# Feed-forward activations turned by VectorE squares and by transfers between SBUF tiles, with the weight blocks in a new order

## The chip, the cores and the metric

One core of a Trainium2 chip runs the whole program. TensorE multiplies (its results go to PSUM, eight banks of 128x512 floats), ScalarE and VectorE work element by element, GpSimd takes a few powers, SyncE issues the loads; 16 DMA engines move the data. The metric is the time of one execution on the device in microseconds, the median of several runs.

## The reference, cut to what matters

Two transformer blocks over 256 tokens of width 1024. Four times in it stands the same feed-forward, twice with an RMS norm ahead of it and a factor of one half, twice in the second block:

```python
def swiglu(u, w_gate, w_up, w_down):
    return (jax.nn.silu(u @ w_gate) * (u @ w_up)) @ w_down
```

Its hidden width is 2816. The rest (latent and differential attention, a recurrent and a convolutional mixer, pooling, cross attention to 256 memory tokens) is not touched by the change, apart from the normalization of the memory tokens, which both kernels spread over the first feed-forward.

## The kernel before, in words

All weights come as a stream of 128x1024 float blocks of 512 KB. Each is loaded by SyncE into one of seven raw buffers (`w_raw`), split by ScalarE into a rounded part (`w_hi`, `part_hi`, L650) and by VectorE into the remainder (`w_lo`, `part_lo`, L1223), and used by TensorE as three products, high x high, high x low, low x high (`three`, L2067 to L2069). The split parts lie in a ring of five (`RING`). ScalarE and VectorE call `behind(b)` in the order of the stream: it splits block b + 5, and ScalarE's part waits until TensorE is done with the block whose place it takes. Each engine works through its queue strictly in order, so whatever stands ahead of a split delays it.

A feed-forward (`token_ffn(f, b0)`, f = 0 to 3) has its hidden width in six pieces n: five of 512 and one of 256. For a piece, TensorE computes gate n into PSUM banks 0 and 1 (one for each half t of the tokens) and up n into banks 2 and 3, four weight blocks each. ScalarE takes silu of the gate (`sig`, L737), VectorE multiplies it with the up result (`hidden`, L1402 and L1403) into `hf`, with tokens on the partitions. The down product needs hidden features on the partitions. So TensorE transposes `hf` by an identity in squares of 128x128 into banks 2 and 3 (`turn_h`, L2318), eight a piece and four for the last; ScalarE copies them into `h_hi` (`hidden_hi`, L743), VectorE makes `h_lo` (`hidden_lo`), and four blocks of down n follow. The order of blocks is written into `ffn_place`: for n = 1 to 4 gate n, down n-1, up n, with `turn_h(n-1)` after the second gate block, and at the end gate 5 with up 5 in one (blocks 56 to 59) and the last six down blocks.

In the queues of the first feed-forward stand also the work on the memory tokens (`memory_stats`, `memory_norm`, `turn_memory`, L2242, `memory_gain`), and of the second one a norm of an embedding (`embedding_sum`, `embedding_var`, whose statistics TensorE sums in L2353, before the second half of gate 1). In the third and fourth, `residual_rows` (VectorE, L1526 and L1529) and `residual_in` (ScalarE, L717) stand ahead of the splits of up 0.

Of the kernel before, what the change touches and what calls it, by code (L numbers as in the profile page):

```python
# [12 lines left out]
ACT = mybir.ActivationFunctionType  # L13
# [3 lines left out]
P = 128  # L17
# [36 lines left out]
FFN_LO = (2,) * 5 + (1,)  # L54
FFN_LO_ALL = sum(FFN_LO)


def ffn_place(kind, n, i=0):

    if n == 0 and kind != "D":  # L60
        return i + (4 if kind == "U" else 0)
    if kind == "D":
        return 8 + 12 * n + 4 + i if n < 4 else 60 + i
    if n < 5:
        return 8 + 12 * (n - 1) + (8 if kind == "U" else 0) + i
    return 56 + i
# [118 lines left out]
def build(nc, x_d, first_d, mem_d, pT, prm_d, id_d, cst_d, late_d, row_d, w_d, out):  # L185
    with ExitStack() as ctx:
# [199 lines left out]
        mem_in, p_in, prm_in, cst_in, out_done, ones_set = sems("mem_in p_in prm_in cst_in out_done ones_set")  # L386
        f_sg, f_h, f_t, f_hh, f_hl = sems("f_sg f_h f_t f_hh f_hl")
        xt_ready, xt_ps, ss_ready, rs_ready, dg_ready, rb_ps, rb_ready = sems(
# [251 lines left out]
        def _(act):  # L640
# [79 lines left out]
            def token_ffn(f, b0):  # L720
# [48 lines left out]
                for n in range(1, 5):  # L769
                    behind(b1 + ffn_place("G", n, 0))  # L770
                    behind(b1 + ffn_place("G", n, 1))
                    hidden_hi(n - 1)
                    if f == 0 and n == 4:
                        memory_hi()
                    behind(b1 + ffn_place("G", n, 2))
                    behind(b1 + ffn_place("G", n, 3))
                    sig(n)
                    for i in range(4):
                        behind(b1 + ffn_place("D", n - 1, i))
                        if f == 0 and n in (2, 3) and i == 1:  # L780
                            memory_gain(n - 2)
                    for i in range(4):
                        behind(b1 + ffn_place("U", n, i))
                        if f == 0 and n == 1 and i == 1:
                            memory_norm()
                behind(b1 + 56)
                hidden_hi(4)
                behind(b1 + 57)
# [3 lines left out]
                behind(b1 + 60)  # L792
                hidden_hi(5)
                for i in range(61, 64):
# [407 lines left out]
        def _(dve):  # L1202
# [195 lines left out]
            def token_ffn(f, b0):  # L1398
# [6 lines left out]
                def hidden(n):  # L1405
                    done(b1 + ffn_place("U", n, 3))
                    if n:
                        dve.wait_ge(f_t, FFN_LO_ALL * f + 2 * n)
                    for t in range(2):
                        dve.wait_ge(f_sg, 12 * f + 2 * n + t + 1)  # L1410
                        times(hf[:, t, :], PB[2 + t][:, :], t, sg[:, t, :]).then_inc(f_h, 1)

                def last_hidden():

                    dve.wait_ge(f_t, FFN_LO_ALL * f + 10)
# [25 lines left out]
                for n in range(1, 5):  # L1441
                    if f == 1 and n == 1:
                        embedding_sum()
                    behind(b1 + ffn_place("G", n, 0))
                    behind(b1 + ffn_place("G", n, 1))
                    hidden_lo(n - 1)
# [9 lines left out]
                    behind(b1 + ffn_place("G", n, 3))  # L1456
                    for i in range(4):
# [7 lines left out]
                    for i in range(3):  # L1465
                        behind(b1 + ffn_place("U", n, i))
                    hidden(n)
                    behind(b1 + ffn_place("U", n, 3))
                behind(b1 + 56)
                hidden_lo(4)  # L1470
# [4 lines left out]
                hidden_lo(5)  # L1475
                behind(b1 + 60)
# [578 lines left out]
        def _(pe):  # L2055
# [202 lines left out]
            def token_ffn(f, b0):  # L2258
# [43 lines left out]
                def up(n):  # L2302
                    if n:
                        pe.wait_ge(f_hl, FFN_LO_ALL * f + 2 * n)
                    if f == 0 and n in (2, 3):
                        pe.wait_ge(mem_g, 4 * (n - 1))
                    for i in range(4):
                        front("U", n, i)

                def turn_h(n):  # L2310
                    pe.wait_ge(f_h, 12 * f + 2 * n + 2)
                    if f == 0 and n == 0:
                        pe.wait_ge(prm_in, 32)
                    for k in range(FFN_LO[n]):
                        for j in range(2):
                            for t in range(2):
                                at = j * S + t * P
                                ins = nc.tensor.transpose(PB[2 + k][:, at:at + P], hf[:, t, (2 * k + j) * P:(2 * k + j + 1) * P], ident)  # L2318
                        ins.then_inc(f_t, 1)

                def down(b, n, jp, h):
                    pe.wait_ge(f_hl, FFN_LO_ALL * f + 2 * n + jp + 1)
                    outs = [PB[k] for k in Y_BANK[y][2 * h:2 * h + 2]]
# [24 lines left out]
                for n in range(1, 5):  # L2348
                    gate(n, 0)
                    gate(n, 1)  # L2350
                    if f == 1 and n == 1:
                        pe.wait_ge(pp_sum, 1)
                        nc.tensor.matmul(half(4, 0), ones, pp_sq[:, 0, :], start=True, stop=True).then_inc(pp_stat, 1)  # L2353
                    turn_h(n - 1)
                    gate(n, 2)
                    gate(n, 3)
                    if f == 1 and n == 1:
                        pe.wait_ge(pp_var, 1)
                    for i in range(4):
                        if f == 0 and n in (2, 3) and i == 2:  # L2360
                            turn_memory(n - 2)
                        down(b1 + ffn_place("D", n - 1, i), n - 1, i // 2, i % 2)
                    up(n)
                gate(5, 0)
                turn_h(4)
                gate(5, 1)
                gate(5, 2)
                token_last(place("G", 5, 3), PB[0:2], (6, 7), x_hi, x_lo, f_gu)
                for i, (n, jp, h) in enumerate(FFN_END):
                    if i < 3 or f < 2:  # L2370
                        down(b1 + 60 + i, n, jp, h)
                    if i == 0:
                        turn_h(5)
                    if i == 3 and f < 2:
# [634 lines left out]
```

## Time and profile before

| | before |
|---|---|
| median of 3 runs, us | 1238.38 (1238.14 to 1238.65) |
| span of the profiled execution, us | 1236.5 |
| TensorE busy, us | 1227.8 (99%) |
| TensorE weight load busy, us | 1046.1 (85%) |
| VectorE busy, us | 801.5 (65%) |
| ScalarE busy, us | 672.9 (54%) |
| moved by DMA | 219.93 MB, mean 178 GB/s |

The page gives for each engine the time with an instruction under way. Matmuls overlap in their pipeline, so a matmul's own duration is more than what it adds to the time; the chain of waits and the starts in the timeline show the latter. Idle time is put down to what ended it.

### The profile page before, as it was taken

The page shows a single profiled execution, that of the slowest core. Times are in us where ns is not written, and L with a number is a line of the kernel's source. Part 1 is how long each engine was busy: PE and PEld are TensorE (multiplying, and loading weights), DVE is VectorE, ACT ScalarE, POOL GpSimd, SP SyncE. Part 2 cuts the span into 40 slices and gives each one's busy share as a digit, 9 for nine tenths or more (in the row PEclk, how much of TensorE's full clock was granted, in tenths as well). Part 3 has the DMA queues.
Part 4 walks back from the last instruction along what each step waited for, and adds up shares of the span by engine and source line. Part 5 has one row for each costly group of instructions (what it writes and reads, how often), then busy time and mean ns, then how long its engine had stood idle before and what let it go on. Part 6 is the DMA issues. An engine that isn't in the chain of part 4 may idle for free.

```text
span 1236.5 us, 16493 instructions
## 1 busy us (share of the span) xinstructions
PE 1227.8 (99%) x6444; PEld 1046.1 (85%) x6444; DVE 801.5 (65%) x1186; ACT 672.9 (54%) x1037; POOL 31.0 (3%) x36
## 2 busy tenths in 40 slices
PE   9999999999999999999999999999999999999997
PEld 8888888888888888899978888888888888888886
DVE  6655556878766555568999765755557674755455
ACT  7545546668574444455776646544445754644441
POOL 0000000010000000000001000000001000000000
PEclk9999999999999999999999999999999999999999
DMA  9755555452355555544445633755554443566540
GB/s 361 260 198 189 187 185 198 156 190 87 110 181 190 189 187 187 187 154 162 167 150 171 214 110 118 268 186 189 188 188 158 172 152 120 204 221 192 188 166 34
DMA packets 60892, 219.93 MB, mean 178 GB/s; under 512 B 6672, under 2 KB 8208, under 8 KB 60176
## 3 DMA queue, kind: packets, MB, share of 16 engines
q1 hardware_dynamic: 60528, 218.50, 51.8%
q8 instruction: 51, 0.84, 0.3%
q10 hardware_dynamic: 288, 0.39, 0.1%
q14 instruction: 25, 0.20, 0.1%
HBM read 217.81 MB, written 1.05 MB: 177 GB/s over the span
## 4 chain that ended last, share of the span: by engine, by line
PE 92%; DVE 6%; issue 1%; DMA 0%; ACT 0%; DVEq 0%; ACTq 0%
PE bank L2067 26%; PE bank L2069 26%; PE bank L2068 26%; PE bank L2119 2%; DVE arena L1881 2%; PE bank L2318 2%; PE bank L2120 1%; DVE w_lo L1223 1%; PE bank L2467 1%; PE bank L2428 1%; PE bank L2288 1%; DVE arena L1896 1%; PE bank L2439 1%; PE bank L2422 1%; PE bank L2460 1%
## 5 line engine op out<-in xcount | busy, mean ns | idle before, releaser
L1223 DVE TENSOR_TENSOR w_lo<-w_raw,w_hi 128x1024 fp32r<-128x1024 f32 x389 | 476.5, 1232 | 339.9 <-ACT w_hi L650 339.1
L650 ACT ACTIVATE w_hi<-w_raw 128x1024 fp32r<-128x1024 f32 x389 | 409.2, 1058 | 422.5 <-PE bank L2069 405.4
L2067 PE MATMUL bank<-w_hi,x_hl 128*128 128x512 f32 (+2 forms) x912 | 357.8, 392 | 0.6 <-DVE w_lo L1223 0.6
L2069 PE MATMUL bank<-w_hi,x_hl 128*128 128x512 f32 (+2 forms) x912 | 353.0, 387 | 0.0
L2068 PE MATMUL bank<-w_lo,x_hl 128*128 128x512 f32 (+2 forms) x912 | 352.8, 387 | 0.0
L2069 PEld LDWEIGHTS bank<-w_hi,x_hl 128*128 128x128 f32 x912 | 171.3, 188 | 34.8
L2067 PEld LDWEIGHTS bank<-w_hi,x_hl 128*128 128x128 f32 x912 | 171.4, 188 | 34.6 <-issue 1.3
L2068 PEld LDWEIGHTS bank<-w_lo,x_hl 128*128 128x128 f32 x912 | 171.5, 188 | 32.9
L2067 PE MATMUL bank<-w_hi,h_hi 128*128 128x512 f32 (+1 forms) x364 | 142.0, 390 | 0.0
L2069 PE MATMUL bank<-w_hi,h_lo 128*128 128x512 f32 (+1 forms) x364 | 141.3, 388 | 0.0
L2068 PE MATMUL bank<-w_lo,h_hi 128*128 128x512 f32 (+1 forms) x364 | 141.2, 388 | 0.0
L2069 PEld LDWEIGHTS bank<-w_hi,h_lo 128*128 128x128 f32 x364 | 68.3, 188 | 14.0
L2067 PEld LDWEIGHTS bank<-w_hi,h_hi 128*128 128x128 f32 x364 | 68.4, 188 | 13.8 <-DVE h_lo L1241 0.2
L2068 PEld LDWEIGHTS bank<-w_lo,h_hi 128*128 128x128 f32 x364 | 68.4, 188 | 13.6
L2119 PE MATMUL bank<-x_hl,w_hi 128*128 128x512 f32 x128 | 46.8, 407 | 0.0
L2067 PE MATMUL bank<-x_hl,w_hi 128*128 128x256 f32 x152 | 43.6, 287 | 0.0
L2068 PE MATMUL bank<-x_hl,w_hi 128*128 128x256 f32 x152 | 43.0, 283 | 0.0
L2069 PE MATMUL bank<-x_hl,w_lo 128*128 128x256 f32 x152 | 43.0, 283 | 0.0
L2067 PE MATMUL bank<-m_hi,w_hi 128*128 128x256 f32 x128 | 37.6, 294 | 0.0
L2068 PE MATMUL bank<-m_lo,w_hi 128*128 128x256 f32 x128 | 36.2, 283 | 0.0
L2069 PE MATMUL bank<-m_hi,w_lo 128*128 128x256 f32 x128 | 36.2, 283 | 0.0
L2120 PE MATMUL bank<-x_hl,w_lo 128*128 128x256 f32 x128 | 35.9, 280 | 0.0
(329 smaller groups left out, 1387.8 us busy)
## 6 DMA issues: line engine op xcount, KB each, us to landing
w_raw<-weights_d SPq DMA_DIRECT2D x394, 512.0 KB, 3.3
arena<-ln_rows_d SPq DMA_DIRECT2D x3, 1024.0 KB, 5.5
arena<-weights_d SPq DMA_DIRECT2D x4, 512.0 KB, 5.2
arena<-late_d SPq DMA_DIRECT2D x1, 1056.0 KB, 7.3
arena<-first_d SPq DMA_DIRECT2D x2, 512.0 KB, 5.5
xs<-x_d SPq DMA_DIRECT2D x2, 512.0 KB, 7.2
kv_mem<-mem_d SPq DMA_DIRECT2D x1, 1024.0 KB, 7.3
out_d<-kv_mem SPq DMA_DIRECT2D x3, 256.0 KB, 2.1
```

What stands on the lines that cost most here:

```text
L650: nc.scalar.activation(w_hi[:, slot(b), :], w_raw[:, b % RAW, :], ACT.Copy).then_inc(hi_ready, 1)
L1223: nc.vector.tensor_tensor(w_lo[:, slot(b), :], w_raw[:, b % RAW, :], w_hi[:, slot(b), :].bitcast(F32), ALU.subtract).then_inc(lo_ready, 1)
L1881: ins = nc.vector.scalar_tensor_tensor(conv[:, c, :], src, w, conv[:, c, :], ALU.mult, ALU.add)
L1896: nc.vector.tensor_tensor(flat(conv), flat(conv), flat(tap_buf[j]), ALU.add).then_inc(tap_added, 1)
L2067: nc.tensor.matmul(out, wh, xh, start=start, stop=False, skip_group_check=True)
L2068: nc.tensor.matmul(out, wh, xl, start=False, stop=False, skip_group_check=True)
L2069: return nc.tensor.matmul(out, wl, xh, start=False, stop=stop, skip_group_check=True)
L2119: nc.tensor.matmul(bank[:, :], wh, flat(x_hl[:, k, :, :]), start=k == 0, stop=k == TILES - 1, skip_group_check=True)
L2120: return nc.tensor.matmul(bank[:, 0:S], wl, x_hl[:, k, 0, :], start=False, stop=k == TILES - 1, skip_group_check=True)
L2288: ins = nc.tensor.matmul(PB[t][:, :], xa[:, c, t * P:(t + 1) * P], wa[:, b, o], start=c == 0 and kind == "high", stop=c == 7 and kind == " ...
L2318: ins = nc.tensor.transpose(PB[2 + k][:, at:at + P], hf[:, t, (2 * k + j) * P:(2 * k + j + 1) * P], ident)
L2422: ins = nc.tensor.matmul(half(n % 2, t), q_mla[0:QK, h, t * P:(t + 1) * P], k_mla[0:QK, h, :], start=True, stop=True)
```

## The change

For the pieces n = 0 to 4, TensorE's transposes go. VectorE turns `hf` in squares of 32x32 (two instructions a piece, one for each t) into `h_quads`. A square is then on the right columns but within its own quarter of the partitions, so ScalarE issues 16 transfers a piece from its own DMA queue (`hidden_across`), each of 32 partitions x 1 KB from a quarter of `h_quads` to a quarter of `h_turned`, both in SBUF. `hidden_hi` waits for all 16 (`h_in`) and copies from there to `h_hi`, in two instructions of 128x512, and `hidden_lo` makes `h_lo` likewise. The piece of 256 is still turned by TensorE (`turn_last`).

The order of blocks becomes gate n, up n, down n-1. ScalarE issues the transfers of piece n after the split behind the first block of down n-1, and copies to `h_hi` after the fourth; for n = 0 the issues come after the first block of gate 1 and the copy after `sig(1)`. The memory tokens' steps move within the first feed-forward, and `turn_memory` waits for the products instead of for `h_lo`.

```diff
     if kind == "D":
-        return 8 + 12 * n + 4 + i if n < 4 else 60 + i
+        return 8 + 12 * n + 8 + i if n < 4 else 60 + i
     if n < 5:
-        return 8 + 12 * (n - 1) + (8 if kind == "U" else 0) + i
+        return 8 + 12 * (n - 1) + (4 if kind == "U" else 0) + i
...
+        h_quads = [region(ARENA - 8 * S if f < 2 else 16 * S, QUADS, 2, 4 * QUAD)[0] for f in range(4)]
+        h_turned = [region(ARENA - 4 * S if f < 2 else 20 * S, QUADS, 2, 4 * QUAD)[0] for f in range(4)]
...
+        def hidden_from(f, t):
+
+            return h_turned[f][:, :, t, :].rearrange("p q (c s) -> p q c s", s=QUAD)
+
+        def hidden_to(h, t):
+
+            return h[:, 0:4, t * P:(t + 1) * P].rearrange("p c (q s) -> p q c s", s=QUAD)
...
                 def hidden_hi(n):
-                    for k in range(FFN_LO[n]):
-                        act.wait_ge(f_t, FFN_LO_ALL * f + 2 * n + k + 1)
-                        j = 2 * k + (4 if n == 5 else 0)
-                        nc.scalar.activation(flat(h_hi[:, j:j + 2, :]), PB[2 + k][:, :], ACT.Copy).then_inc(f_hh, 1)
+                    act.wait_ge(h_in, 16 * QUADS * QUADS * (TURNED * f + n + 1))
+                    if n:
+                        done(b1 + ffn_place("D", n - 1, 3))
+                    for t in range(2):
+                        nc.scalar.activation(hidden_to(h_hi, t), hidden_from(f, t), ACT.Copy).then_inc(f_hh, 1)
+
+                def hidden_across(n):
+                    act.wait_ge(h_turn, 2 * (TURNED * f + n + 1))
+                    for q in range(QUADS):
+                        for r in range(QUADS):
+                            nc.scalar.dma_start(h_turned[f][r * QUAD:(r + 1) * QUAD, q, :, :], h_quads[f][q * QUAD:(q + 1) * QUAD, r, :, :]
+                                                ).then_inc(h_in, 16)
...
                 for n in range(1, 5):
-                    behind(b1 + ffn_place("G", n, 0))
-                    behind(b1 + ffn_place("G", n, 1))
-                    hidden_hi(n - 1)
-                    if f == 0 and n == 4:
-                        memory_hi()
-                    behind(b1 + ffn_place("G", n, 2))
-                    behind(b1 + ffn_place("G", n, 3))
+                    for i in range(4):
+                        behind(b1 + ffn_place("G", n, i))
+                        if n == 1 and i == 0:
+                            hidden_across(0)
+                        if f == 0 and n == 2 and i == 1:
+                            memory_norm()
+                        if f == 0 and n == 4 and i == 1:
+                            memory_hi()
                     sig(n)
+                    if n == 1:
+                        hidden_hi(0)
+                    for i in range(4):
+                        behind(b1 + ffn_place("U", n, i))
                     for i in range(4):
                         behind(b1 + ffn_place("D", n - 1, i))
+                        if i == 0:
+                            hidden_across(n)
                         if f == 0 and n in (2, 3) and i == 1:
                             memory_gain(n - 2)
...
+                    hidden_hi(n)
...
                 def hidden(n):
                     done(b1 + ffn_place("U", n, 3))
-                    if n:
-                        dve.wait_ge(f_t, FFN_LO_ALL * f + 2 * n)
                     for t in range(2):
                         dve.wait_ge(f_sg, 12 * f + 2 * n + t + 1)
                         times(hf[:, t, :], PB[2 + t][:, :], t, sg[:, t, :]).then_inc(f_h, 1)
+                    if TURNED * f + n:
+                        dve.wait_ge(h_in, 16 * QUADS * QUADS * (TURNED * f + n))
+                    for t in range(2):
+                        dve.wait_ge(f_h, 12 * f + 2 * n + t + 1)
+                        nc.vector.transpose(h_quads[f][:, :, t, :].rearrange("p r (c s) -> p c r s", s=QUAD),
+                                            hf[:, t, :].rearrange("p (c r j) -> p c r j", r=QUADS, j=QUAD)).then_inc(h_turn, 1)
...
-                    for k in range(FFN_LO[n]):
-                        dve.wait_ge(f_hh, FFN_LO_ALL * f + 2 * n + k + 1)
-                        j = 2 * k + (4 if n == 5 else 0)
-                        low(flat(h_lo[:, j:j + 2, :]), PB[2 + k][:, :], flat(h_hi[:, j:j + 2, :]), f_hl)
+                    for t in range(2):
+                        dve.wait_ge(f_hh, FFN_LO_ALL * f + 2 * n + t + 1)
+                        low(hidden_to(h_lo, t), hidden_from(f, t), hidden_to(h_hi, t), f_hl)
...
             def turn_memory(h):
 
                 pe.wait_ge(mem_xn, 4)
-                pe.wait_ge(f_hl, 2 * (h + 2))
+                pe.wait_ge(f_h, 2 * (h + 2) + 2)
...
                 def up(n):
                     if n:
-                        pe.wait_ge(f_hl, FFN_LO_ALL * f + 2 * n)
+                        pe.wait_ge(f_h, 12 * f + 2 * n)
...
-                    turn_h(n - 1)
                     gate(n, 2)
                     gate(n, 3)
+                    up(n)
                     if f == 1 and n == 1:
                         pe.wait_ge(pp_var, 1)
                     for i in range(4):
                         if f == 0 and n in (2, 3) and i == 2:
                             turn_memory(n - 2)
                         down(b1 + ffn_place("D", n - 1, i), n - 1, i // 2, i % 2)
-                    up(n)
                 gate(5, 0)
-                turn_h(4)
                 gate(5, 1)
```

## Rows read from the trace of the kernel before

**Rows 1.** Busy time, its share of the span, and instructions of each engine.

```profile
PE 1227.8 (99%) x6444; PEld 1046.1 (85%) x6444; DVE 801.5 (65%) x1186; ACT 672.9 (54%) x1037; POOL 31.0 (3%) x36
```

**Rows 2.** TensorE's waits: line, released by, us in total, times, longest.

```profile
PE bank L2531 <- POOL tokst L588: 1.0, 1, 1.0
PE bank L2067 <- DVE w_lo L1223: 0.6, 1, 0.6
PE bank L2288 <- ACT w_hi L927: 0.5, 1, 0.5
```

**Rows 3.** Busy time by stretches, columns in the first line.

```profile
core 0: us, PE busy (x) PEld busy (x) DVE busy (x) ACT busy (x) POOL busy (x), PEclk, DMA share, GB/s
62.00:95.54 33.54, 33.54 (x158) 27.96 (x157) 17.30 (x17) 16.23 (x20) 0.00 (x0) 1.00 0.62 208
95.54:129.10 33.56, 33.56 (x158) 27.95 (x157) 16.85 (x21) 16.67 (x20) 0.00 (x0) 1.00 0.55 178
...
444.50:478.06 33.56, 33.56 (x154) 27.86 (x153) 18.83 (x21) 14.88 (x17) 0.00 (x0) 1.00 0.55 188
```

**Rows 4.** The activations' transposes (L2318): duration in ns, minimum, median, maximum.

```profile
L2318 PE MATMUL bank<-ident,arena x176: 270/272/276, 33.2 to 1216.0; 128*128 128x128 f32 x176
```

**Rows 5.** Chain that ended last: start, us on the chain, what.

```profile
33.15 0.23 PE bank L2069
33.38 0.87 PE bank L2318 x8
34.26 0.23 PE bank L2067
...
415.91 0.88 PE bank L2318 x8
449.44 0.87 PE bank L2318 x8
```

**Rows 6.** Timeline of ScalarE in feed-forward 0: start, us, instruction, idle before it.

```profile
96.00 1.06 ACT L650 ACTIVATE w_hi<-w_raw 128x1024 fp32r<-128x1024 f32 x1 [1.66 <-PE bank L2069]
98.72 1.06 ACT L650 ACTIVATE w_hi<-w_raw 128x1024 fp32r<-128x1024 f32 x1 [1.66 <-PE bank L2069]
```

**Rows 7.** Timeline of VectorE in the same stretch, and products in feed-forward 2.

```profile
95.94 1.41 DVE L1403 SCALAR_TENSOR_TENSOR arena<-bank,tokst,arena 128x512 f32<-128x512 f32 x2 [0.34 <-PE bank L2069]
...
99.81 1.23 DVE L1223 TENSOR_TENSOR w_lo<-w_raw,w_hi 128x1024 fp32r<-128x1024 f32 x1 [1.33 <-ACT w_hi L650]
...
815.66 1.29 DVE L1402 TENSOR_TENSOR arena<-bank,arena 128x512 f32<-128x512 f32 x2 [0.34 <-PE bank L2069]
```

**Rows 8.** Groups of instructions by form: busy us, mean ns of one, idle before.

```profile
L1953 DVE COPY arena<-bank 128x128 f32<-128x128 f32 x2 | 0.5, 282 | 0.0
...
L1241 DVE TENSOR_TENSOR h_lo<-bank,h_hi 128x512 fp32r<-128x512 f32 x44 | 28.4, 683 | 5.1 <-ACT h_hi L743 5.1
L1241 DVE TENSOR_TENSOR m_lo<-kv_mem,m_hi 128x512 fp32r<-128x512 f32 x4 | 2.5, 684 | 0.0
L1896 DVE TENSOR_TENSOR arena<-arena 128x1024 f32<-128x1024 f32 x10 | 12.2, 1221 | 0.3
```

**Rows 9.** Issues of transfers: durations in ns, back-to-back issues, KB and us to landing.

```profile
L1026 ACTq DMA_DIRECT2D arena<-pT_d x1: 378/378/378, 325.4 to 325.4; - x1
L1199 ACTq DMA_DIRECT2D out_d<-kv_mem x1: 353/353/353, 1233.9 to 1233.9; - x1
L579 SPq DMA_DIRECT2D w_raw<-weights_d x391: 327/328/738, 3.8 to 1198.4; - x196
0.74 0.86 SPq L544 DMA_DIRECT2D arena<-first_d  x2
w_raw<-weights_d SPq DMA_DIRECT2D x394, 512.0 KB, 3.3
out_d<-kv_mem ACTq DMA_DIRECT2D x1, 128.0 KB, 2.2
```

**Rows 10.** Timeline of VectorE, then of TensorE, at the start of feed-forward 1's loop.

```profile
376.51 1.41 DVE L1403 SCALAR_TENSOR_TENSOR arena<-bank,tokst,arena 128x512 f32<-128x512 f32 x2 [0.34 <-PE bank L2069]
380.95 0.43 DVE L1305 TENSOR_TENSOR arena<-arena 128x256 f32<-128x256 f32 x1
381.76 0.59 PE L2353 MATMUL bank<-arena,ones 128*128 128x256 f32 x2
```

**Rows 11.** Timeline of VectorE and ScalarE at the start of feed-forward 2's loop.

```profile
784.76 1.28 DVE L1402 TENSOR_TENSOR arena<-bank,arena 128x512 f32<-128x512 f32 x2
784.90 1.06 ACT L650 ACTIVATE w_hi<-w_raw 128x1024 fp32r<-128x1024 f32 x1 [0.74 <-PE bank L2069]
```

**Rows 12.** Timeline of VectorE around the memory statistics in feed-forward 0.

```profile
47.49 2.46 DVE L1328 BATCH_NORM_STATS2 tokst<-kv_mem 128x6 f32<-128x512 f32 x4
49.98 0.28 DVE L1331 BATCH_NORM_AGGREGATE tokst<-tokst 128x2 f32<-128x12 f32 x2
50.30 0.17 DVE L1333 TENSOR_SCALAR tokst<-tokst 128x2 f32<-128x2 f32 x1
```

More of the change, by code:

```diff
@@ L55 @@
 FFN_LO_ALL = sum(FFN_LO)
+TURNED = 5
+QUADS = 4
+QUAD = P // QUADS
 def ffn_place(kind, n, i=0):
@@ L386, in build @@
         mem_in, p_in, prm_in, cst_in, out_done, ones_set = sems("mem_in p_in prm_in cst_in out_done ones_set")
-        f_sg, f_h, f_t, f_hh, f_hl = sems("f_sg f_h f_t f_hh f_hl")
+        f_sg, f_h, f_t, f_hh, f_hl, h_turn, h_in = sems("f_sg f_h f_t f_hh f_hl h_turn h_in")
         xt_ready, xt_ps, ss_ready, rs_ready, dg_ready, rb_ps, rb_ready = sems(
@@ L739, in hidden_hi, with last_hidden_hi @@
                 def hidden_hi(n):
-                    for k in range(FFN_LO[n]):
-                        act.wait_ge(f_t, FFN_LO_ALL * f + 2 * n + k + 1)
-                        j = 2 * k + (4 if n == 5 else 0)
-                        nc.scalar.activation(flat(h_hi[:, j:j + 2, :]), PB[2 + k][:, :], ACT.Copy).then_inc(f_hh, 1)
+                    act.wait_ge(h_in, 16 * QUADS * QUADS * (TURNED * f + n + 1))
[9 more added lines that the diff above has]
+                                                ).then_inc(h_in, 16)
+                def last_hidden_hi():
+                    act.wait_ge(f_t, f + 1)
+                    nc.scalar.activation(flat(h_hi[:, 4:6, :]), PB[2][:, :], ACT.Copy).then_inc(f_hh, 1)
                 for i in range(AHEAD if f >= 2 else 0, 4):
@@ L792, in token_ffn @@
                 behind(b1 + 60)
-                hidden_hi(5)
+                last_hidden_hi()
                 for i in range(61, 64):
@@ L1420, in hidden_lo, with last_hidden_lo @@
                 def hidden_lo(n):
-                    for k in range(FFN_LO[n]):
-                        dve.wait_ge(f_hh, FFN_LO_ALL * f + 2 * n + k + 1)
-                        j = 2 * k + (4 if n == 5 else 0)
-                        low(flat(h_lo[:, j:j + 2, :]), PB[2 + k][:, :], flat(h_hi[:, j:j + 2, :]), f_hl)
+                    for t in range(2):
+                        dve.wait_ge(f_hh, FFN_LO_ALL * f + 2 * n + t + 1)
+                        low(hidden_to(h_lo, t), hidden_from(f, t), hidden_to(h_hi, t), f_hl)
+                def last_hidden_lo():
+                    dve.wait_ge(f_hh, FFN_LO_ALL * (f + 1))
+                    low(flat(h_lo[:, 4:6, :]), PB[2][:, :], flat(h_hi[:, 4:6, :]), f_hl)
                 for i in range(AHEAD if f >= 2 else 0, 4):
@@ L1445, in token_ffn @@
                     behind(b1 + ffn_place("G", n, 1))
-                    hidden_lo(n - 1)
                     if f == 0 and n == 3:
@@ L1456, in token_ffn @@
                     behind(b1 + ffn_place("G", n, 3))
+                    if n == 1:
+                        hidden_lo(0)
+                    for i in range(3):
+                        behind(b1 + ffn_place("U", n, i))
+                    hidden(n)
+                    behind(b1 + ffn_place("U", n, 3))
                     for i in range(4):
@@ L1464, in token_ffn @@
                             embedding_norm(n, i)
[L1465 to L1468, printed above, removed]
+                    hidden_lo(n)
                 behind(b1 + 56)
-                hidden_lo(4)
                 behind(b1 + 57)
@@ L1474, in token_ffn @@
                 behind(b1 + 59)
-                hidden_lo(5)
+                last_hidden_lo()
                 behind(b1 + 60)
@@ L2238, in turn_memory @@
                 pe.wait_ge(mem_xn, 4)
-                pe.wait_ge(f_hl, 2 * (h + 2))
+                pe.wait_ge(f_h, 2 * (h + 2) + 2)
+                if h == 0:
+                    pe.wait_ge(prm_in, 32)
                 for c in range(4 * h, 4 * h + 4):
@@ L2303, in up, with turn_last @@
                     if n:
-                        pe.wait_ge(f_hl, FFN_LO_ALL * f + 2 * n)
-                    if f == 0 and n in (2, 3):
-                        pe.wait_ge(mem_g, 4 * (n - 1))
+                        pe.wait_ge(f_h, 12 * f + 2 * n)
+                    if f == 0 and n in (3, 4):
+                        pe.wait_ge(mem_g, 4 * (n - 2))
                     for i in range(4):
                         front("U", n, i)
[L2310 to L2319, printed above, removed]
+                def turn_last():
+                    pe.wait_ge(f_h, 12 * (f + 1))
+                    for j in range(2):
+                        for t in range(2):
+                            at = j * S + t * P
+                            ins = nc.tensor.transpose(PB[2][:, at:at + P], hf[:, t, j * P:(j + 1) * P], ident)
+                    ins.then_inc(f_t, 1)
                 def down(b, n, jp, h):
-                    pe.wait_ge(f_hl, FFN_LO_ALL * f + 2 * n + jp + 1)
+                    pe.wait_ge(f_hl, FFN_LO_ALL * f + 2 * n + (1 if n == 5 else 2))
                     outs = [PB[k] for k in Y_BANK[y][2 * h:2 * h + 2]]
@@ L2372, in token_ffn @@
                     if i == 0:
-                        turn_h(5)
+                        turn_last()
                     if i == 3 and f < 2:
```

7 lines of the change are left out of this document (1 added, 6 removed).

## The prediction

> **What bounds the kernel now.** I read the page's busy shares first: TensorE 1227.8 us of a span of 1236.5, VectorE 801.5, ScalarE 672.9 [rows 1]. A busy TensorE row may hide overlaps, so next its waits, and there are three in the whole execution, 2.1 us together, none in a feed-forward stage [rows 2]. The table by stretches shows PE busy through all of two iterations of a feed-forward loop at a granted clock of 1.00 [rows 3]. So only two things move the time: instructions taken from TensorE's queue, and new waits in it.
>
> **What is removed.** `turn_h` turned each 128x512 pair of activation tiles with 8 transposes (L2318), 176 in all: 4 feed-forwards x (5 x 8 + 4) [rows 4]. The change keeps the last 4 of each, so 160 go, in 20 groups of 8. Their own 272 ns is a pipelined duration and not their price. The chain of waits gives the price: 0.87 us for 8, where each matmul around them has 0.23 [rows 5]. The starts agree: from the group at 415.91 to that at 449.44 is 33.53 us, for 144 matmuls (12 blocks x 12) and one group. A block takes 2.72 us by ScalarE's steps (96.00 to 98.72) [rows 6]; 12 are 32.64, which leaves 0.89. So 20 x 0.875 = **17.5 us**, straight off the bounding engine. The Trainium skill ("VectorE: DVE Perf Modes", The three transpose paths) prices a TensorE transpose at 390 ns, for 2-byte data; by it 160 would give 62 us. The chain shows 109 ns each in this kernel, and the sum goes by that.
>
> **The new path and its cover.** For n = 1 to 4, set t = 0 where up n ends. TensorE then has down n-1 (4 blocks, D0 to D3), gate n+1 (G0 to G3) and up n+1 (U0 ...) before it needs the activations of n: 12 blocks, 32.6 us. For n = 0 it is gate 1 and up 1, 21.8 us. In between come:
> - VectorE: two products, 1.29 or 1.41 us as a pair, beginning 0.34 us after up ends [rows 7], as before; then two transposes in 32x32 squares of 128x512 each. No row shows one. From below: a copy of 128x128 takes 0.28 us; from above: a 128x1024 instruction takes 1.22 [rows 8]. I take 0.69, the rows of plain 128x512 instructions, since the element count is the same. Ready at t = 0.34 + 1.41 + 1.38 + 0.1 = 3.2. (The same page of the Trainium skill gives 311 ns for 128x128 in 2-byte data; 4 of these would be 1.24 us, about the upper end.)
> - ScalarE: at D0's end it splits one weight block (2.8 to 3.9 [rows 6]), and then `hidden_across` issues 16 transfers from its own queue. This is the large new cost, and what is queued behind it is the split of G2. Single issues from ScalarE took 0.38 and 0.35 us; from SyncE 0.33 in the median; SyncE's first two, back to back, 0.86 for 2; single ones up to 0.74 while many 512 KB loads were under way [rows 9]. I take 0.45 each, the back-to-back row and its gap, as the transfers here are 32 KB; ends 0.33 and 0.78 (0.74 and a gap). 16 x 0.45 = 7.2 us, until t = 11.1.
> - The cover: the split of G2 must be complete when TensorE begins G2, 6 blocks after t = 0, at 16.3. From ScalarE's start to VectorE's end such a pair takes 2.32 us (98.72 to 101.04) [rows 6, 7]. So ScalarE may begin as late as 14.0, and the 16 issues may take 14.0 - 3.9 = **10.1 us, or 0.63 each**. With 7.2, 2.9 us are to spare. Afterwards ScalarE needs 1.06 and VectorE 1.23 us a block against TensorE's 2.72, and the lag is gone within three blocks.
> - Landing: a load of 512 KB takes 3.3 us and the 128 KB store from ScalarE's queue 2.2 [rows 9]. Last issue at 11.1, all in at about 14. `hidden_hi(n)` stands behind the split of U0, at 14.3, so it hardly waits. It may be late: the split of U1 behind it must begin by 24.5 - 2.3 = 22.2, so with its own 1.07 the data may come at 21.1. The extra traffic is 0.5 MB in 32.6 us, beside 6.3 MB of weights, with the DMA engines 55 to 62% busy [rows 3].
> - ScalarE's load per iteration becomes 14.9 to 16.7 + 7.2, at most 24 of 32.6 us; VectorE's 17 to 19 + 1.4 [rows 3]. Neither becomes the bound. The squares and the copies to `h_hi` and `h_lo` keep their number and element count (2 of 128x512 each); they read SBUF instead of PSUM, and plain 128x512 instructions of either source take 0.68 to 0.69 on VectorE [rows 8].
>
> For n = 0 the same reckoning holds with G0's end at 2.8: the split of U2 behind the issues is needed at 16.3 as well. `sig(1)` and `hidden_hi(0)` then come at 13.5 to 16.1 and `hidden_lo(0)` ends by 18, for a need at 21.8.
>
> **Places with less cover.** (a) Feed-forward 1, n = 1: `embedding_sum` is on VectorE behind `hidden(0)`, and TensorE's statistics matmul (L2353, at 381.76) waits for it; it ended at 381.38 [rows 10]. The transposes put 1.38 + 0.1 us ahead of it, of which 0.38 is covered: **+1.1 us** once (0.3 with transposes of 0.28, 2.2 with 1.22). (b) Feed-forwards 2 and 3, n = 0: `residual_rows` makes VectorE late, and its products began at 784.76, 2.6 us after up 0 ended (782.1, from the release at 784.90) [rows 11]. The issues begin at 787.5 instead of 786.0: with 7.2 us the split of U2 ends 797.1 for a need at 798.4. Nothing at 0.45; 1.0 us twice at 0.60. (c) Feed-forward 0, n = 1: `memory_stats` puts 3 us on VectorE between two splits [rows 12]. Here G3 is the tight block: about 17.6 for 19.0. Nothing. (d) The memory transposes wait for `f_h` instead of `f_hl`; at D1's end, 5.4, the products have been done for 3.7 us. Nothing. (e) Gate, up and `sig` wait for products that now lie eight blocks back. Nothing, given the row of waits. The last blocks of each feed-forward keep their order, and SyncE's loads wait for split blocks at most 6 us later than now, with seven raw buffers ahead: a load for D1 issued at 13.5 lands at 17 for a split at 24.5.
>
> **Sum.** -17.5 + 1.1 = -16.4 us. The profiled execution spans 1236.5 us, the median of three is 1238.4, which is 1.9 us around it; I leave that unchanged. 1238.4 - 16.4 = **1222.0 us** (span 1220.1). Its own range is 1220.3 (statistics wait covered, transposes cheap) to 1224 (transposes dear and stall (b)).
>
> **Rivals.**
> 1. The issues are dear, and ScalarE's queue becomes the bound. For: 16 in a row is a burst that the trace never shows, and one issue took 0.74. Against: both issues from this queue took 0.35 and 0.38. Above 0.63 each, TensorE stalls 20 times by (16p - 10.1); the gain is gone at 16p = 10.1 + 0.87, p = 0.69. At 0.78: 20 x 2.4 = 48 us, **1270 us**. Chance 8%.
> 2. Transfers one after the other. If each of 16 took the 2.2 us of the small store before the next moved, the data would be in at 3.9 + 35 = 39; the split of U1 would be complete at 42.5 for a need at 24.5, 18 us x 20: **near 1580 us**. Chance 2%. Against it stand 0.86 us for two issues and loads that land in 3.3 us although their packets share 16 engines. The Trainium skill speaks for it: "DMA: Bandwidth & Descriptors" (Rules for kernel authors) calls transfers under 64 KB mostly overhead and wants them joined; these are 32 KB. Its overhead would be latency, for which the cover of 10 us is there.
> 3. Partial stalls: issues of 0.5 to 0.65, or transposes above 1.3, or landing pushed behind weight loads, so that the tight places and some iterations lose 0.2 to 0.6 us each. 3 to 11 us: **1225 to 1233**. Chance 12%.
> 4. The stretch is emptied, but TensorE doesn't run sooner: the change does not do what it says, because another resource sets the pace of its matmuls and lets the clock or the 0.23 us slip. For: nothing but that PE is 99% busy. Against: granted clock 1.00 in every stretch. **1236 to 1240**. Chance 3%.
>
> **How the numbers follow.** 75% for the forecast. The range for 8 in 10 takes the forecast's range, a little below it for a gain that I have not seen, and the larger part of rival 3: 1219.5 to 1230. About 0.2%, 2.5 us, is what a measurement can tell from no change. Faster 0.87 (forecast and rival 3), same 0.04 (rival 4 and rival 1 just at its threshold), slower 0.09 (rivals 1 and 2).
>
> **What would show it.** In the changed kernel's profile: 16 rows of L2318; the feed-forward period 32.65 us (33.53 less 0.88); each burst of ScalarE issues 6 to 9 us long and over by t = 13; a VectorE transpose near 0.69; one wait of TensorE before L2353 of about 1.1 us, and no waits for `w_lo` in the loops. Waits of matmuls for `w_lo`, once an iteration at G2 (U2 for n = 0), mean rival 1 or 3; ScalarE idle before the `h_hi` copy until a DMA means landing, rival 2; a period above 32.65 without waits means rival 4.

## The result and the profile after

| | before | after |
|---|---|---|
| median, us | 1238.28 (1238.14 to 1238.65) | 1231.07 (1230.83 to 1231.76) |
| span of the profiled execution, us | 1236.5 | 1229.2 |

The ratio of after to before is 0.9942, with a 95% interval of 0.9928 to 0.9956. The kernel is 7.2 us faster; the forecast was 16.4 us and 1222.0, with 1230 as the upper end of the range. The direction held, the gain is less than half of the one forecast, and the time lies 1.1 us above the range.

The page of after, busy time of each engine [rows 1]:

```profile
PE 1212.3 (99%) x6284; PEld 1028.5 (84%) x6284; DVE 815.1 (66%) x1226; ACT 664.1 (54%) x1037; POOL 31.0 (3%) x36
```

TensorE has 160 instructions fewer, as the change says. Its waits (line, released by, total, times, longest) stand against the three of [rows 2]:

```profile
PE bank L2103 <- DVE w_lo L1251: 7.9, 7, 1.6
PE bank L2564 <- POOL tokst L601: 1.0, 1, 1.0
PE bank L2326 <- ACT w_hi L955: 0.8, 1, 0.8
PE bank L2388 <- DVE arena L1333: 0.7, 1, 0.7
```

Six of the seven waits for `w_lo` are new, and the one on L2388 is new too. Where none of them lies, the removed work shows in full: this stretch of after runs from the end of up 2 to that of up 3 in feed-forward 2 (columns as in [rows 3]), and is 32.64 us for 12 blocks. Before, the same 12 blocks with their group of transposes took 33.53 (449.44 - 415.91 in [rows 5]).

```profile
834.72:867.36 32.64, 32.64 (x146) 27.03 (x144) 17.84 (x18) 14.18 (x16) 0.00 (x0) 1.00 0.62 211
```

The new instructions: VectorE's transposes and ScalarE's issues (durations in ns, minimum, median, maximum), then the groups by form of the copies that now read SBUF [rows 8].

```profile
L1442 DVE STREAM_TRANSPOSE arena<-arena x40: 669/688/707, 31.7 to 1186.1; 128x512 f32<-128x512 f32 x40
L763 ACTq DMA_DIRECT2D arena<-arena x320: 514/612/1524, 33.0 to 1196.6; - x160
...
L757 ACT ACTIVATE h_hi<-arena 128x512 fp32r<-128x512 f32 x40 | 22.8, 619 | 0.0
...
L1269 DVE TENSOR_TENSOR h_lo<-arena,h_hi 128x512 fp32r<-128x512 f32 x40 | 25.8, 687 | 0.1
```

An issue takes 0.61 us where 0.45 was assumed. Below, "row" is the uninterrupted series of 16 issues of one piece. Three such rows in ScalarE's timeline of after show what that does. Each line is a start, a duration and an instruction. The first row is of feed-forward 2, piece 2, with a split ahead of it and one behind it; the second is of feed-forward 3, piece 1, and the third of feed-forward 0, piece 0.

```profile
837.70 1.06 ACT L663 ACTIVATE w_hi<-w_raw 128x1024 fp32r<-128x1024 f32 x1 [1.66 <-PE bank L2105]
837.72 10.44 ACTq L763 DMA_DIRECT2D arena<-arena  x16
848.26 1.06 ACT L663 ACTIVATE w_hi<-w_raw 128x1024 fp32r<-128x1024 f32 x1 [9.50 <-issue]
...
1088.37 11.45 ACTq L763 DMA_DIRECT2D arena<-arena  x16
...
33.00 10.44 ACTq L763 DMA_DIRECT2D arena<-arena  x16
43.54 2.95 ACT L663 ACTIVATE w_hi<-w_raw 128x1024 fp32r<-128x1024 f32 x3 [11.63 <-issue]
```

In the first, up 2 had ended at 834.72, so the row begins at t = 3.0, in step with the split and not behind it; the next split begins at 13.5 and TensorE does not wait. In the second, up 1 had ended at 1084.46; the row begins at 3.9 and is 11.45 long, because one issue in it takes 1.52 us (the maximum above). In the third, up 0 had ended at 27.9, and the row begins at 5.1, because VectorE's products came late. TensorE's timeline at the third, and at the second:

```profile
43.96 0.39 PE L2105 MATMUL bank<-w_hi,x_hl 128*128 128x512 f32 x1
45.91 0.50 PE L2103 MATMUL bank<-w_hi,x_hl 128*128 128x512 f32 x1 [1.56 <-DVE w_lo L1251]
46.25 0.39 PE L2104 MATMUL bank<-w_lo,x_hl 128*128 128x512 f32 x1
...
1102.29 0.50 PE L2103 MATMUL bank<-w_hi,x_hl 128*128 128x512 f32 x1 [1.35 <-DVE w_lo L1251]
```

A wait costs more than the idle time shown. From 43.96 to 46.25 are 2.29 us for two steps of 0.227, so 1.84 us are lost where 1.56 are shown as idle: the idle time is counted from the modelled end of the matmul before, and the first one behind a stall is slower. Reckoned like this, the six waits, which start at 44, 68, 71, 794, 1077 and 1101 us, cost 1.84, 0.64, 1.29, 1.75, 1.78 and 1.63, together 8.9 us. One late row makes the next one late: VectorE is still catching up, and after the stall of piece 0 the products of piece 1 begin 1.4 us after up 1 instead of 0.34 (the line is of feed-forward 3, where up 1 ended at 1084.46), and so the row of piece 1 begins late.

```profile
1085.85 1.28 DVE L1430 TENSOR_TENSOR arena<-bank,arena 128x512 f32<-128x512 f32 x2
```

In feed-forward 2, piece 1, the row begins at about 3.7 for this reason, and 0.30 us are lost at 817.84 (the next two starts are 818.26 and 818.60), which the list of waits does not show.

### The profile page after: what moved, and what is told of

Same layout as the page of the kernel before. It is cut to its first block, busy times and chain, and to the rows that moved or that the text cites. A ratio compares the mean times of both kernels' runs of the same rounds, so it can differ in the third digit from the quotient of the medians.

```text
span 1229.2 us, 16567 instructions
## 1 busy us (share of the span) xinstructions
PE 1212.3 (99%) x6284; PEld 1028.5 (84%) x6284; DVE 815.1 (66%) x1226; ACT 664.1 (54%) x1037; POOL 31.0 (3%) x36
## 2 busy tenths in 40 slices
DMA packets 76255, 230.45 MB, mean 187 GB/s; under 512 B 11792, under 2 KB 23568, under 8 KB 75536
## 4 chain that ended last, share of the span: by engine, by line
PE 78%; DVE 11%; ACTq 4%; ACT 3%; issue 2%; DMA 1%; SPq 0%; POOL 0%; DVEq 0%
PE bank L2103 22%; PE bank L2105 22%; PE bank L2104 22%; ACTq L763 4%; DVE w_lo L1251 4%; PE bank L2155 2%; DVE arena L1917 2%; PE bank L2156 1%; ACT w_hi L663 1%; PE bank L2500 1%; PE bank L2461 1%; DVE arena L1932 1%; DMA w_raw<-weights_d 1%; PE bank L2472 1%; ACT xs L843 1%
## 5 line engine op out<-in xcount | busy, mean ns | idle before, releaser
L1251 DVE TENSOR_TENSOR w_lo<-w_raw,w_hi 128x1024 fp32r<-128x1024 f32 x389 | 468.0, 1227 | 319.5 <-ACT w_hi L663 316.8
L663 ACT ACTIVATE w_hi<-w_raw 128x1024 fp32r<-128x1024 f32 x389 | 401.5, 1055 | 422.2 <-PE bank L2105 239.1
L2103 PEld LDWEIGHTS bank<-w_hi,x_hl 128*128 128x128 f32 x912 | 171.2, 188 | 45.6 <-DVE w_lo L1251 10.5
```

The source lines that it names most:

```text
L663: nc.scalar.activation(w_hi[:, slot(b), :], w_raw[:, b % RAW, :], ACT.Copy).then_inc(hi_ready, 1)
L1251: nc.vector.tensor_tensor(w_lo[:, slot(b), :], w_raw[:, b % RAW, :], w_hi[:, slot(b), :].bitcast(F32), ALU.subtract).then_inc(lo_ready, 1)
L2103: nc.tensor.matmul(out, wh, xh, start=start, stop=False, skip_group_check=True)
```

## The experiments

Theory A: the uninterrupted row of 16 issues in ScalarE's queue makes the six waits. Rivals: B, the added traffic or VectorE's added work delays the splits; C, the new order of blocks costs the time. All ratios are to the kernel before, on the same chip. The diffs are cut to the lines that matter; what else was moved is said beside them.

**One row of 16 split into four of 4 (spread4).**

```diff
-                def hidden_across(n):
-                    act.wait_ge(h_turn, 2 * (TURNED * f + n + 1))
-                    for q in range(QUADS):
-                        for r in range(QUADS):
+                def hidden_across(n, q):
+                    if q == 0:
+                        act.wait_ge(h_turn, 2 * (TURNED * f + n + 1))
+                    for r in range(QUADS):
...
                         behind(b1 + ffn_place("D", n - 1, i))
-                        if i == 0:
-                            hidden_across(n)
+                        hidden_across(n, i)
```

ScalarE's copy to `h_hi` and VectorE's `hidden_lo` come later in their queues, as the transfers now end later.

> The changed kernel, but ScalarE issues the 16 transfers of a piece in four groups of 4, one behind each of four weight splits, and copies to h_hi two splits later than before. Theory A (the uninterrupted row of 16 issues, 10.1 to 11.5 us against a cover of 10.1, makes the six new waits for w_lo): a group takes 4 x 0.63 = 2.5 us, the waits for w_lo in the feed-forwards vanish, only the 0.7 us before L2388 stays with about 0.3 us of restart; 1238.3 - 17.5 + 1.0 = 1221.8 us. Rival B (the added traffic delays the weight loads, or VectorE's transposes delay the splits): both are still there, waits stay near 7 us, 1231 us.

1221.63 us, ratio 0.9866 (0.985 to 0.9883). No wait for `w_lo` is left in the feed-forwards, with the same transfers and the same VectorE work, so both halves of B fall as the cause of the waits. That it is not the moved copies that help is seen in the next run, where they stay where they were. ScalarE's timeline of this kernel shows the groups beside the splits:

```profile
398.04 1.06 ACT L663 ACTIVATE w_hi<-w_raw 128x1024 fp32r<-128x1024 f32 x1 [1.66 <-PE bank L2108]
398.06 2.44 ACTq L763 DMA_DIRECT2D arena<-arena  x4
400.75 1.06 ACT L663 ACTIVATE w_hi<-w_raw 128x1024 fp32r<-128x1024 f32 x1 [1.66 <-PE bank L2108]
400.77 2.44 ACTq L763 DMA_DIRECT2D arena<-arena  x4
403.48 1.06 ACT L663 ACTIVATE w_hi<-w_raw 128x1024 fp32r<-128x1024 f32 x1 [1.66 <-PE bank L2108]
```

Four issues take 2.44 us and begin 0.02 us after the split, which runs on. Both fit into one block of 2.72, so the splits stay in step with TensorE and nothing is delayed at all.

**Half of the issues (half_issues).**

```diff
-                    for q in range(QUADS):
+                    for q in range(2):
                         for r in range(QUADS):
```

The semaphore counts follow the number of transfers.

> The changed kernel with only 8 of the 16 transfers of a piece (q = 0 and 1), in one row; the other half of the turned activations is left out, and the copies read old values there. One extra load of 512 KB near the start gives that place a content. Theory A: a row takes 8 x 0.63 = 5.1 us, no wait for w_lo in the feed-forwards, 1221.8 us as in the spread kernel. Rival C (the new block order itself costs the time): 1231 us. Rival B's half on VectorE: 1231 us; its half on traffic: about 1227 us.

1221.70 us, ratio 0.9867 (0.9852 to 0.9881). A row is 5.0 us, and the block order and the place of the copies are those of after: C falls.

**The order of blocks alone (order_only).** The kernel before with the new `ffn_place`, the loops of all three engines in that order, and `turn_h(n - 1)` still behind `gate(n, 1)`. The memory tokens' steps move with the blocks.

```diff
-        return 8 + 12 * n + 4 + i if n < 4 else 60 + i
+        return 8 + 12 * n + 8 + i if n < 4 else 60 + i
...
-        return 8 + 12 * (n - 1) + (8 if kind == "U" else 0) + i
+        return 8 + 12 * (n - 1) + (4 if kind == "U" else 0) + i
...
                     gate(n, 3)
+                    up(n)
...
                         down(b1 + ffn_place("D", n - 1, i), n - 1, i // 2, i % 2)
-                    up(n)
```

> The kernel before with the new block order alone: gate n, up n, down n-1, with TensorE's transposes of the activations still behind the second gate block. Theory A: nothing is removed and nothing waits, 1238.3 us within 0.5. Rival C: the order costs about 10 us, 1248 us.

1238.20 us, ratio 1.000 (0.9991 to 1.0009). With TensorE's transposes still in place, the order neither costs nor saves anything.

**All issues from SyncE (sync_issues).** `hidden_across` is taken out of ScalarE's queue, and SyncE issues the row ahead of the load that lies 12 blocks later (`turned_at`).

```diff
             for b in range(4, NB):
+                if b in turned_at:
+                    f, n = turned_at[b]
+                    sp.wait_ge(h_turn, 2 * (TURNED * f + n + 1))
+                    for q in range(QUADS):
+                        for r in range(QUADS):
+                            sp.dma_start(h_turned[f][r * QUAD:(r + 1) * QUAD, q, :, :], h_quads[f][q * QUAD:(q + 1) * QUAD, r, :, :]
+                                         ).then_inc(h_in, 16)
```

> The changed kernel with the 16 transfers of a piece issued in one row by SyncE instead of ScalarE, ahead of its load 12 blocks later. Theory A: ScalarE's queue is free again, no waits for w_lo in the feed-forwards, the wait before L2388 stays: 1221.8 us, and ScalarE's copy to h_hi waits for the landing at most 4 us, hidden. If an issue on SyncE costs 0.33 us, the 0.61 us is a matter of ScalarE's queue; if it costs 0.6 as well, of the transfer's form or of a burst. Rival B (traffic, or loads that are now delayed by the row on SyncE): waits for w_lo or for weight loads of 5 us or more, 1228 to 1233 us.

1221.46 us, ratio 0.9865 (0.985 to 0.9879). An issue costs 0.59 us on SyncE too (the first line below), so the price is not one of ScalarE's queue. ScalarE's copies now wait for the landing, 74.9 us over 20 pieces (the group, with its idle time), and that costs nothing:

```profile
L572 SPq DMA_DIRECT2D arena<-arena x320: 507/591/1614, 33.7 to 1188.5; - x160
...
L770 ACT ACTIVATE h_hi<-arena 128x512 fp32r<-128x512 f32 x40 | 23.1, 625 | 74.9 <-DMA arena<-arena 74.9
```

The Trainium skill ("Trainium Kernel Development and Optimization", Key Constraints) says that issuing from several engines concurrently only saves the sequencer's issue time. By that rule, the trace agrees: 230.45 MB are moved in both kernels, and taking the issues out of ScalarE's queue gave back 9.6 us, which covers the 8.9 us of the waits for `w_lo`.

**Four more issues in each row (more_issues).** The counts for which ScalarE and VectorE wait are raised to 20 as well.

```diff
+                    for r in range(QUADS):
+                        nc.scalar.dma_start(idle_rows[r * QUAD:(r + 1) * QUAD, :, :], h_quads[f][0:QUAD, r, :, :]).then_inc(h_in, 16)
```

> The changed kernel with 20 issues in each row instead of 16: four more transfers of 32 partitions x 1 KB into a tile that nobody reads. Theory A, with the cover as the trace of the changed kernel shows it: a row takes 20 x 0.634 = 12.7 us. In an ordinary piece it begins 3.0 us after up n ends (it is dispatched while the split is still under way), so ScalarE's next split begins at 15.8 where 14.0 is free of cost: a stall of 1.8 + 0.1 us in 13 pieces that now have none; the 6 or 7 pieces whose row begins at 3.9 to 5.3 lose 2.5 us more than now. 1231 + 25 + 16 = 1272 us, between 1262 and 1278. Rival B (traffic or VectorE): a quarter more traffic, about 1233 us.

1284.46 us, ratio 1.0366 (1.0342 to 1.039): slower than before, and above the range of theory A, whose forecast was 1272. An ordinary piece loses what it should: the gap between matmul starts is 2.1 us where 0.23 is normal, and 1.9 was forecast. What the forecast left out is the clock. The stretches of this kernel around its longest stall, around an ordinary one (109 to 111), and around two of middle length (columns as in [rows 3]; the granted clock is the third value from the end):

```profile
44.00:48.30 4.30, 0.10 (x1) 0.00 (x0) 1.21 (x2) 2.30 (x3) 0.00 (x0) 0.82 0.15 38
48.30:52.00 3.70, 3.63 (x9) 2.86 (x10) 3.58 (x5) 3.70 (x7) 0.00 (x0) 0.50 0.64 189
52.00:56.00 4.00, 4.00 (x16) 3.25 (x15) 3.39 (x3) 2.09 (x3) 0.00 (x0) 0.81 0.91 330
56.00:60.00 4.00, 4.00 (x20) 3.30 (x19) 3.64 (x6) 1.73 (x2) 0.00 (x0) 1.00 0.83 274
109.00:111.00 2.00, 0.71 (x4) 0.25 (x2) 1.18 (x1) 2.00 (x4) 0.00 (x0) 1.00 0.06 16
...
179.00:183.20 4.20, 1.77 (x8) 1.16 (x7) 2.28 (x2) 3.37 (x4) 0.00 (x0) 1.00 0.09 23
183.20:187.00 3.80, 3.80 (x11) 2.93 (x11) 3.80 (x6) 2.59 (x5) 0.00 (x0) 0.55 0.91 286
...
1147.00:1152.00 5.00, 2.64 (x12) 1.86 (x11) 3.06 (x3) 4.15 (x6) 0.00 (x0) 1.00 0.23 57
```

After the stall that ended at 48.37 the granted clock is 0.50, the lower level of 1.2 GHz, until about 53.5, with 0.43 us a matmul instead of 0.23. The trace has seven such stretches. Four lie at the longest stalls, with 3.2 to 4.3 us of idle time, and three follow stalls with 2.43, 2.50 and 1.88 us (TensorE resumes at 182.20, 541.01 and 1219.71), while stalls with 2.36 us (at 1150.22, the last line above) and 1.91 us (at 853.84) have none behind them. Matmul starts set against those of spread_sum, which has no such stalls, give 2.2, 1.6, 2.4, 1.6, 1.4, 2.3 and 1.6 us for the slow matmuls, about 13 us beside the stalls themselves. The profiled execution took 1286.76 us, 14.8 above the forecast, so the clock is most of the miss. The four executions go the same way: mean granted clocks of 0.986, 0.987, 0.990 and 0.991 belong to 1286.8, 1287.4, 1282.2 and 1281.3 us.

**What sets the price of an issue.** Four kernels change the transfers alone.

flat_rows, one run of 256 floats a partition instead of 2 x 128:

```diff
-nc.scalar.dma_start(h_turned[f][r * QUAD:(r + 1) * QUAD, q, :, :], h_quads[f][q * QUAD:(q + 1) * QUAD, r, :, :]
+nc.scalar.dma_start(h_turned[f][r * QUAD:(r + 1) * QUAD, q, :, :].rearrange("p a b -> p (a b)"), h_quads[f][q * QUAD:(q + 1) * QUAD, r, :, :].rearrange("p a b -> p (a b)")
```

> The changed kernel with source and destination of each transfer written as one run of 256 floats a partition instead of 2 x 128, the same bytes. If the number of dimensions sets an issue's price, it falls from 0.61 to about 0.35 us, a row to 6 us, and the time to 1221.8 us; if not, an issue stays at 0.61 and the time at 1231 us.

1231.34 us, ratio 0.9943 (0.9928 to 0.9958), an issue 0.612: the pattern's dimensions have no part in it.

half_rows, 16 partitions a transfer:

```diff
-nc.scalar.dma_start(h_turned[f][r * QUAD:(r + 1) * QUAD, q, :, :], h_quads[f][q * QUAD:(q + 1) * QUAD, r, :, :]
+nc.scalar.dma_start(h_turned[f][r * QUAD:r * QUAD + 16, q, :, :], h_quads[f][q * QUAD:q * QUAD + 16, r, :, :]
```

> The changed kernel with 16 transfers of 16 partitions x 1 KB a piece instead of 32 partitions; the other half of the turned activations is left out, and one extra load near the start gives that place a content. If the price is one of each issue, it stays at 0.61 us and the time at 1231; if it follows the rows, it falls to 0.35 to 0.45 and the time to about 1222.

One run, 1231.07 us, an issue 0.611. With half the bytes in each transfer the time is that of after, which also speaks against the traffic. whole_rows, four transfers of 128 partitions:

```diff
                     for q in range(QUADS):
-                        for r in range(QUADS):
-                            nc.scalar.dma_start(h_turned[f][r * QUAD:(r + 1) * QUAD, q, :, :], h_quads[f][q * QUAD:(q + 1) * QUAD, r, :, :]
-                                                ).then_inc(h_in, 16)
+                        nc.scalar.dma_start(h_turned[f][:, q, :, :], h_quads[f][:, q, :, :]).then_inc(h_in, 64)
```

> The changed kernel with 4 transfers of 128 partitions x 1 KB a piece instead of 16 of 32 partitions; nothing crosses a quarter of the partitions, so the activations are not fully turned (left out). Same bytes. Theory A: a row takes at most 4 x 0.63 = 2.5 us, if the price is one of each issue and not of its rows, and the time is 1221.8 us. If an issue's price follows its descriptors, one takes about 4 x 0.6 = 2.4 us and the time stays at 1231.

One run, 1221.52 us, an issue 0.622. So 16, 32 or 128 partitions cost the issuer the same within 0.01 us, and a row of four issues is hidden.

from_dram, the source in DRAM:

```diff
-nc.scalar.dma_start(h_turned[f][r * QUAD:(r + 1) * QUAD, q, :, :], h_quads[f][q * QUAD:(q + 1) * QUAD, r, :, :]
+nc.scalar.dma_start(h_turned[f][r * QUAD:(r + 1) * QUAD, q, :, :], w_d[20][q * QUAD:(q + 1) * QUAD, r * 256:(r + 1) * 256].rearrange("p (a b) -> p a b", b=128)
```

> The changed kernel with 16 transfers of 32 partitions x 1 KB a piece whose source is a weight block in DRAM instead of h_quads; the turned activations are left out. If the SBUF source sets the 0.61 us of an issue, it falls to the 0.35 us of ScalarE's two loads and stores with DRAM, a row to 6 us, and the time to 1221.8; if not, 0.61 and 1231.

One run, 1221.22 us. Issues in whole_rows and in from_dram:

```profile
L762 ACTq DMA_DIRECT2D arena<-arena x80: 485/622/2131, 32.9 to 1179.7; - x80
...
L763 ACTq DMA_DIRECT2D arena<-weights_d x320: 317/443/1397, 33.5 to 1184.4; - x160
```

With a source in DRAM an issue in a row costs 0.44 us, and with its gaps 0.47 to 0.52 (rows of 7.5 to 8.4 us), close to the 0.45 that the prediction took from [rows 9], where every transfer has DRAM on one side. With SBUF on both sides it costs 0.61. Why is not shown.

The slow issue of feed-forward 3, piece 1, is not an accident of one execution. The rows of this piece in flat_rows and in half_rows:

```profile
1088.83 11.37 ACTq L763 DMA_DIRECT2D arena<-arena  x16
...
1088.51 11.29 ACTq L767 DMA_DIRECT2D arena<-arena  x16
```

In all three kernels the third issue of this row, at 1089.6 to 1090.0 us, takes 1.4 to 1.5 us, and TensorE then waits 1.2 to 1.4 us for `w_lo` (until 1102.3 to 1102.7). What makes it slow at this place is not shown.

**The wait of L2388 (spread_sum, sync_sum).** VectorE's `embedding_sum` ahead of the transposes of piece 0 in feed-forward 1, in the spread kernel and in the one with SyncE's issues.

```diff
-                hidden(0)
+                products(0)
+                if f != 1:
+                    squares(0)
                 behind(b1 + ffn_place("U", 0, 3))
                 for n in range(1, 5):
                     if f == 1 and n == 1:
                         embedding_sum()
+                        squares(0)
```

> The spread kernel (4 issues behind each of four splits), and in feed-forward 1 VectorE does embedding_sum ahead of the two transposes of piece 0 instead of behind them. The 0.7 us wait of TensorE before its statistics matmul goes, with 0.3 us of restart: 1221.6 - 1.0 = 1220.6 us, the full 17.5 us below before. If something else now waits in its place (the issues of piece 0 begin 3.6 us later), a wait for w_lo shows there and the time stays near 1221.6.

1220.44 us, ratio 0.9855 (0.984 to 0.9869).

> The kernel with all issues on SyncE, and the same move of embedding_sum. 1221.5 - 1.0 = 1220.5 us; its row for piece 0 of feed-forward 1 begins 3.6 us later, which delays weight loads that have more than 10 us to spare.

1220.49 us, ratio 0.9854 (0.9837 to 0.987). Both are 1.0 to 1.2 us below their parents, and no run of one overlaps the runs of its parent, though they were taken on different occasions; the wait of L2388 is gone from both profiles. TensorE's waits in spread_sum are those of [rows 2] less one:

```profile
PE bank L2576 <- POOL tokst L601: 1.0, 1, 1.0
PE bank L2115 <- DVE w_lo L1252: 0.6, 1, 0.6
```

These two are the fastest kernels of the study, 17.8 and 17.9 us below before.

## Why the prediction was right or wrong

- **What bounds the kernel, and the 17.5 us.** Right. The period is 32.64 us for 32.65; with every new wait removed the gain is 17.8 or 17.9.
- **VectorE's transposes.** 0.69 us forecast, 0.688 measured. The estimate of 1.24 from the Trainium skill ("VectorE: DVE Perf Modes", The three transpose paths), its 311 ns for a 128x128 in 2-byte data times four, would have been too much: for this 4-byte 128x512 the measurement decides.
- **An issue's price.** This is the term that failed: 0.45 us, a row of 7.2, against 0.61 and, with the gaps, rows of 10.14 us or more (0.634 each). The row ends at t = 13.1 in an ordinary piece instead of 11.1, and the splits behind it, for which the sum had no stall at all, cost TensorE 9.2 us. The price lay within the ends of 0.33 and 0.78, and on the threshold of 0.63 that the prediction had worked out. Its error was to choose the middle value from rows of another kind of transfer and then to end the range at 1230, inside its own rival 3 (issues of 0.5 to 0.65, 1225 to 1233), which it gave 12% and which happened, with fewer and larger stalls (0.3 to 1.8 us each) than the 0.2 to 0.6 written there.
- **The cover.** 10.1 us was worked out for a row that stands behind the split of D0. The trace of after shows the row dispatched while that split is still running, at t = 3.0, so an ordinary piece covers 11.0 us, and in 14 of 20 pieces TensorE loses nothing at the splits. Two errors went against each other here, and it is luck that only six pieces lose time: with a row begun at 3.9, as reckoned, 0.634 would have used up the whole cover in every piece. more_issues confirms 11.0: with 12.7 us an ordinary piece loses 1.9.
- **The tight places.** Each of the waits goes with a row that began late, and one of them with a row that was also long (it would have lost about 0.3 us, by this estimate from the 11.45 and 10.14, without its slow issue). (b) was called: 1.0 us twice at 0.60 was written, and 1.75 and 1.78 came at 0.634. (c) was called free and cost 0.64 and 1.29: the row begins at 4.0 (55.72, for an up 1 that ended at 51.7), late from the stall of piece 0, and with a row of 10.14 `memory_stats` no longer fits. Feed-forward 0, piece 0, was not named: VectorE's products begin there at 30.35, 2.5 us after up 0, as they did before (30.41), which one more look at the first iteration would have shown; 1.84 us. The sixth, 1.63 us in feed-forward 3, piece 1, comes from a row of 11.45 us begun at 3.9; in before no issue of a transfer takes more than 0.74 us [rows 9]. That a stall in piece 0 makes the row of piece 1 late, 0.30 us more in feed-forward 2, was not foreseen either.
- **(a), the statistics wait.** 1.1 us forecast; 0.7 idle, 0.96 by the starts of the matmuls, and 1.0 to 1.2 by the two kernels without it.
- **The low end of the forecast's own range**, 1220.3, lies 0.6 us below 1238.4 - 17.5, and no term of the prediction says where this comes from.
- **Landing** (2.5 us median), traffic, the order of blocks, the copies from SBUF (VectorE 0.687; ScalarE 0.62 for 0.59 from PSUM): free, as forecast. The weight loads land later, 4.3 us in the median for 3.3 before, but no matmul waits for one in the feed-forwards. Rivals 1, 2 and 4 as written did not happen; rival 1's mechanism did, at its threshold.

The sum as it came: -17.5 + 8.9 + 0.3 + 1.0 = -7.3, for 7.2 measured and 7.3 in the spans.

## What to carry to other kernels

A transfer costs the queue that issues it a time that here did not depend on its size (0.61 to 0.62 us for 16 to 128 KB), and what stands behind it is late by the whole row: compare the row, not one issue, with the slack of the tightest thing behind it, in the iteration where it starts latest. A place that stalls makes the next row late as well. If the row is near that slack, break it up between the instructions that keep the pace, which here cost nothing and gave back 9.4 us, or give it to a queue with nothing urgent in it. When a price has no row of its own kind, the range has to reach as far as the slack's threshold says it matters.

## What the runs showed of the hardware

- An issue with SBUF on both sides takes 0.59 to 0.62 us on ScalarE's and on SyncE's queue, for 16, 32 and 128 partitions of 1 KB; with a DRAM source 0.44 in rows of 16; single ones with DRAM on one side took 0.33 to 0.38 [rows 9]. The Trainium skill ("DMA: Bandwidth & Descriptors", Rules for kernel authors) wants transfers under 64 KB joined as mostly overhead. By that rule the trace agrees for the issuer's time: four transfers of 128 KB (whole_rows) hold the queue for 2.5 us where 16 of 32 KB hold it for 10.1. For landing no run shows it, as no matmul of a down product waited for landing in any kernel here.
- An issue runs beside an ACTIVATE of the same engine that was started before it (0.02 us apart), but the next ACTIVATE waits for the row to end.
- Single issues in a row took up to 1.5 us (2.1 in whole_rows), and in after, flat_rows and half_rows one did so at the same place (1089.6 to 1090.0). Why is not shown.
- In more_issues TensorE's granted clock fell to 0.50 (the level of 1.2 GHz) in seven stretches, about 13 us lost besides the stalls. Four go with idle times of 3.2 to 4.3 us and three with 1.88, 2.43 and 2.50; idle times of 1.91 and 2.36 had none behind them. So the length of the idle time alone does not tell, and what decides is not shown.
- With 10.5 MB more moved in after (230.45 for 219.93 MB), the 512 KB weight loads landed in 4.3 us in the median instead of 3.3.
